# Differential attention, last pair of heads: scores, norms and products in another order among the output projection's units

## The reference, cut

```python
def one(qs):
    a, c = qs
    s1 = jnp.einsum('bhqd,bhkd->bhqk', a, k1).astype(jnp.float32) * scale
    s2 = jnp.einsum('bhqd,bhkd->bhqk', c, k2).astype(jnp.float32) * scale
    p = jax.nn.softmax(s1, axis=-1) - lam * jax.nn.softmax(s2, axis=-1)
    return jnp.einsum('bhqk,bhkv->bhqv', p.astype(v.dtype), v)
...
def post(o):
    return merge_heads(rms_norm(o, subln_g) * (1.0 - lam_init)) @ w_out

yx = post(diff_attend(q1x, q2x, k1a, k2a, va, lam))
...
h_x = h_x + gm * rms_norm(yx, norm_g[l, 1])
fx = conv_ffn(modulate(rms_norm(h_x, norm_g[l, 2]), shf, scf), ...)
```

## Time and profile before

| | us |
|---|---|
| median of 3 runs | 1880.49 (1878.75 to 1881.62) |
| profiled execution | 1877.86 |
| its span, first to last instruction | 1876.1 |
| TensorE busy | 1797.3 |
| VectorE busy | 1142.5 |
| ScalarE busy | 836.0 |
| mean granted clock of TensorE | 0.986 |

### The profile page before, as it was taken

One profiled execution on the slowest core, in us unless ns is written; L12 is line 12 of the kernel. 1 busy time (PEld: TensorE's weight loads), 2 busy tenths in 40 slices (PEclk: granted clock), 3 DMA queues, 4 the chain that ended last, 5 costly groups with the idle time before them and its releaser, 6 DMA issues. The chain is left out here.

```text
span 1876.1 us, 26231 instructions
## 1 busy us (share of the span) xinstructions
PE 1797.3 (96%) x9865; PEld 1501.4 (80%) x9865; DVE 1142.5 (61%) x1523; ACT 836.0 (45%) x1206; POOL 87.0 (5%) x164
## 2 busy tenths in 40 slices
PE   5999999999999999999989999799989999989997
PEld 2877767777678888888878887699879987879985
DVE  2766757667367688644346565566665695755554
ACT  3423233332456432334245555556554546544453
POOL 2000001000000010000000000000001000000000
PEclk8999999999999999999999999899999999999999
DMA  8654545545355476432323223355545554546662
GB/s 290 196 154 143 161 144 151 154 143 159 97 207 186 136 232 184 131 93 97 105 62 107 79 82 99 102 182 185 187 152 183 161 158 146 179 135 186 183 192 100
DMA packets 150910, 282.38 MB, mean 151 GB/s; under 512 B 12652, under 2 KB 78308, under 8 KB 150689
## 3 DMA queue, kind: packets, MB, share of 16 engines
q1 hardware_dynamic: 133344, 220.54, 37.7%
q0 software_dynamic: 17472, 60.57, 10.6%
HBM read 276.83 MB, written 4.23 MB: 150 GB/s over the span
## 5 line engine op out<-in xcount | busy, mean ns | idle before, releaser
L2245 DVE TENSOR_TENSOR wl<-raw,wh 128x1024 fp32r<-128x1024 f32 (+1 forms) x388 | 454.5, 1181 | 379.0 <-ACT wh L1521 376.4
L1521 ACT ACTIVATE wh<-raw 128x1024 fp32r<-128x1024 f32 (+1 forms) x388 | 393.5, 1023 | 614.7 <-PE ps L571 601.5
L569 PE MATMUL ps<-uh,wh 128*128 128x256 f32 (+1 forms) x1216 | 380.7, 313 | 7.3 <-DVE spare L2267 7.3
L570 PE MATMUL ps<-ul,wh 128*128 128x256 f32 (+1 forms) x1216 | 378.9, 312 | 0.0
L571 PE MATMUL ps<-uh,wl 128*128 128x256 f32 (+1 forms) x1216 | 378.8, 311 | 0.0
L569 PE MATMUL ps<-wh,uh 128*128 128x512 f32 (+2 forms) x960 | 368.2, 383 | 9.7 <-issue 6.2
L570 PE MATMUL ps<-wl,uh 128*128 128x512 f32 (+2 forms) x960 | 354.6, 369 | 0.0
L571 PE MATMUL ps<-wh,ul 128*128 128x512 f32 (+2 forms) x960 | 354.3, 369 | 0.0
L569 PEld LDWEIGHTS ps<-uh,wh 128*128 128x128 f32 x1216 | 231.9, 191 | 22.4 <-issue 7.0
L571 PEld LDWEIGHTS ps<-uh,wl 128*128 128x128 f32 x1216 | 231.9, 191 | 12.7
L570 PEld LDWEIGHTS ps<-ul,wh 128*128 128x128 f32 x1216 | 231.9, 191 | 12.3
(11 more groups left out here) (302 smaller groups left out, 1486.9 us busy)
## 6 DMA issues: line engine op xcount, KB each, us to landing
raw<-in_ffn_w_up SPq DMA_DIRECT2D x176, 256.0 KB
arena<-in_ada_w POOLq DMA_DIRECT2D x80, 512.0 KB, 4.2
raw<-in_w_in SPq DMA_DIRECT2D x60, 512.0 KB
raw<-in_ret_w_in SPq DMA_DIRECT2D x48, 512.0 KB
raw<-in_ffn_w_down SPq DMA_DIRECT2D x40, 512.0 KB
raw<-in_ret_w_out SPq DMA_DIRECT2D x32, 512.0 KB
raw<-in_w_up SPq DMA_DIRECT2D x32, 512.0 KB
raw<-in_w_down SPq DMA_DIRECT2D x32, 512.0 KB
```

The source lines that it names most:

```text
L569: pe.matmul(o, lh, rh, start=first, stop=False)
L570: pe.matmul(o, lh, rl, start=False, stop=False)
L1521: T.mark(act.activation(wh[:, j, 0:size], raw[:, j, 0:size], ACT.Copy), hi_done)
L2245: T.mark(vec.tensor_tensor(wl[:, j, 0:size], raw[:, j, 0:size], wh[:, j, 0:size], ALU.subtract), lo_done)
```

## The change

For the last pair (LAST = 3), scores (0, 0) and (0, 1) go ahead of output unit 0, around `values(2)`; `turn_dy(2)` and both scores of head 1 go behind unit 1, with score (1, 0) now in bank 2 and (1, 1) in bank 0 (`score_bank`). The probabilities are turned behind units 2 and 3. The products are taken per head, head 0 behind unit 3 and head 1 behind unit 4, into banks 2 and 3, with a root, a scaling, a transposition (banks 0 and 1) and a pair of high and low parts for each. On ScalarE a function without a reader is called at some places: a root (`roots_next`) ahead of three row norms and behind the last exponents, and an exponential (`exponents_next`) behind the root of pair 2. The reciprocal row sums of the last pair lie in columns of their own (`shares`). On VectorE the helpers `scale_values` and `take_dy` get the heads as a parameter in the same way as on the other engines. Leading blanks are cut, and so are hunks that only pass on the new helpers.

```diff
@@ -343,6 +343,25 @@
 def normed_block(nt, half, b, c):
     x = parts_of(uh, nt, half)[1]
     return x[:, b, c * 256:(c + 1) * 256] if nt == 4 else x[:, 2 * b + c, :]
+def score_bank(i, h, t):
+    return 0 if (h, t) == ((1, 1) if i == LAST else (1, 0)) else 2
+LAST = DH // 2 - 1
+def turned_bank(i, h):
+    return h if i == LAST else 0
+def shares(i, o, n=1):
+    c = (72 if i == LAST else 56) + o
+    return st[:, c:c + n]
+def value_bank(i, h):
+    return 2 + h if i == LAST else h
 def tiles_of(nt, part):
@@ -1097,11 +1116,12 @@
         if (h, t) == (0, 0):
             pe.wait_ge(dqkt_ready, i + 1)
             pe.wait_ge(emptied, values_group[0])
-        elif (h, t) != (1, 0):
-            pe.wait_ge(dexp_done, 4 * i + h + t)
-        elif i:
-            pe.wait_ge(dyt_lo, i)
-        b = heads_v if (h, t) == (1, 0) else heads_v + 2
+        elif score_bank(i, h, t) == 0:
+            if i:
+                pe.wait_ge(dyt_lo, i)
+        else:
+            pe.wait_ge(dexp_done, 4 * i + (2 if (h, t) == (1, 0) else h + t))
+        b = heads_v + score_bank(i, h, t)
         for c in range(2):
             r = slice(64 * c, 64 * c + 64)
             mm = pe.matmul(ps[:, b + c, :], dqt[r, h, t * P:(t + 1) * P], dkt[r, h, :], start=True, stop=True)
@@ -1110,29 +1130,31 @@
     def turn_dprob(i, h, b):
         pe.wait_ge(dprob_ready, 4 * i + 2 * h + 2)
+        if i == LAST:
+            pe.wait_ge(dexp_done, 4 * i + 3 + h)
         for k in range(4):
             for t in range(2):
                 c = (k % 2) * SEQ + t * P
                 mm = pe.transpose(ps[:, b + k // 2, c:c + P], dpr[:, h, t, k * P:(k + 1) * P], ident[:, :])
         mm.then_inc(dprob_turned, 1)
-    def values(i):
-        pe.wait_ge(dpt_ready, 2 * i + 2)
+    def values(i, heads=range(2)):
+        pe.wait_ge(dpt_ready, 2 * i + heads[-1] + 1)
         pe.wait_ge(emptied, values_group[0])
-        for h in range(2):
+        for h in heads:
             for t in range(2):
                 for k in range(4):
-                    mm = pe.matmul(ps[:, heads_v + h, t * P:(t + 1) * P], dpt[:, h, k, t * P:(t + 1) * P],
+                    mm = pe.matmul(ps[:, heads_v + value_bank(i, h), t * P:(t + 1) * P], dpt[:, h, k, t * P:(t + 1) * P],
                                    dvs[i % 2][:, k, h * P:(h + 1) * P], start=k == 0, stop=k == 3)
             mm.then_inc(dvalued, 1)
-    def turn_dy(i):
-        pe.wait_ge(dy_ready, 2 * i + 2)
-        for h in range(2):
+    def turn_dy(i, heads=range(2)):
+        pe.wait_ge(dy_ready, 2 * i + heads[-1] + 1)
+        for h in heads:
             for t in range(2):
-                mm = pe.transpose(ps[:, heads_v, h * SEQ + t * P:h * SEQ + (t + 1) * P], dy[:, h, t, :], ident[:, :])
+                mm = pe.transpose(ps[:, heads_v + turned_bank(i, h), h * SEQ + t * P:h * SEQ + (t + 1) * P], dy[:, h, t, :], ident[:, :])
         mm.then_inc(dy_turned, 1)
     values_group = [0]
@@ -1210,13 +1232,11 @@
             base = S.next() * SLOTS
             for half in (range(0, 2), range(2, 4)):
                 apart = s == 1 and half[0] == 2
-                if apart:
-                    turn_dy(DH // 2 - 1)
                 for z in ((0,), (1,)) if apart else ((0, 1),):
                     for j in half:
                         pe.wait_ge(lo_done, base + j + 1)
                         k = 4 * s + j
-                        pe.wait_ge(dyt_lo, k // 2 + 1)
+                        pe.wait_ge(dyt_lo, LAST + 1 + k % 2 if apart else k // 2 + 1)
                         for t in z:
                             for c in range(2):
                                 mm = three(ps[:, heads_q + 2 * t + c, :], ah8[:, k, t * P:(t + 1) * P], al8[:, k, t * P:(t + 1) * P],
@@ -1242,17 +1262,24 @@
                 pe.wait_ge(dqkt_ready, i + 1)
                 for h in range(2):
                     turn_dprob(i - 1, h, heads_q + 2 * h)
-    last = DH // 2 - 1
+    score(LAST, 0, 0)
+    values(LAST - 1)
+    score(LAST, 0, 1)
     for k in project_heads():
-        if k < 4:
-            attend_early(last, k)
+        if k == 1:
+            turn_dy(LAST - 1)
+            score(LAST, 1, 0)
+            score(LAST, 1, 1)
+        elif k == 2:
+            turn_dprob(LAST, 0, heads_v + 2)
+        elif k == 3:
+            turn_dprob(LAST, 1, heads_v)
+            values(LAST, range(0, 1))
         elif k == 4:
-            pe.wait_ge(dexp_done, 4 * last + 3)
-            turn_dprob(last, 0, heads_v)
-        else:
-            pe.wait_ge(dexp_done, 4 * last + 4)
-            turn_dprob(last, 1, heads_v + 2)
-            values(last)
+            values(LAST, range(1, 2))
+            turn_dy(LAST, range(0, 1))
+        elif k == 5:
+            turn_dy(LAST, range(1, 2))
     turn_normed(2)
     with pe.Fori(0, 5) as i:
         S.enter(i, 2)
@@ -1582,6 +1609,11 @@
             o = part * SEQ
             T.mark(act.activation(ah[:, j, o:o + SEQ], yt[:, 4 * s + j, o:o + SEQ], ACT.Copy), ak_hi)
+    def roots_next():
+        T.settle()
+        T.mark(act.activation(st[:, 71:72], epsc[:, 0:1], ACT.Sqrt), act_own)
     def rms(tiles, src, width, cols, waits=None):
         for t in tiles:
@@ -1885,6 +1917,7 @@
     project(lambda k: hid[:, k, :], TOK, par.now())
     shift0[0] = 0
     layer[0] = 1
+    roots_next()
     act.wait_ge(rows_done, 1)
     for t in range(2):
         square_y(t, side)
@@ -1942,22 +1975,38 @@
         act.wait_ge(dprob_turned, 2 * i + h + 1)
         T.mark(act.activation(dpt[:, h, :, :], ps[:, b:b + 2, :].rearrange("p b (k n) -> p (b k) n", k=2), ACT.Copy), dpt_ready)
-    def rms_values(i):
-        for h in range(2):
+    def square_values(i, heads=range(2)):
+        for h in heads:
             act.wait_ge(dvalued, 2 * i + h + 1)
             for t in range(2):
                 o = 2 * h + t
                 T.settle()
-                T.mark(act.activation(junk[:, 0:P], ps[:, heads_v + h, t * P:(t + 1) * P], ACT.Square,
-                                      scale=st[:, 56 + 2 * o:57 + 2 * o], accum_out=st[:, 16 + o:17 + o]), act_own)
+                T.mark(act.activation(junk[:, 0:P], ps[:, heads_v + value_bank(i, h), t * P:(t + 1) * P], ACT.Square,
+                                      scale=shares(i, 2 * o), accum_out=st[:, 16 + o:17 + o]), act_own)
+    def root_values(heads=range(2)):
         T.settle()
-        T.mark(act.activation(st[:, 20:24], st[:, 16:20], ACT.Sqrt, scale=1.0 / P, bias=epsc[:, 0:1]), drms_done)
-    def take_dy(i):
-        act.wait_ge(dy_turned, i + 1)
-        T.mark(act.activation(ah8[:, 2 * i:2 * i + 2, :], ps[:, heads_v, :].rearrange("p (h n) -> p h n", h=2), ACT.Copy,
+        c = slice(2 * heads[0], 2 * heads[-1] + 2)
+        T.mark(act.activation(st[:, 20:24][:, c], st[:, 16:20][:, c], ACT.Sqrt, scale=1.0 / P, bias=epsc[:, 0:1]), drms_done)
+    def exponents_next():
+        T.settle()
+        T.mark(act.activation(st[:, 70:71], epsc[:, 0:1], ACT.Exp), act_own)
+    def rms_values(i):
+        square_values(i)
+        root_values()
+    def take_dy(i, heads=range(2)):
+        act.wait_ge(dy_turned, i + heads[-1] + 1 if i == LAST else i + 1)
+        k, o = 2 * i + heads[0], heads[0] * SEQ
+        n = len(heads)
+        T.mark(act.activation(ah8[:, k:k + n, :], ps[:, heads_v + turned_bank(i, heads[0]), o:o + n * SEQ].rearrange("p (h n) -> p h n", h=n), ACT.Copy,
                               scale=lamt[:, 5:6]), dyt_hi)
     def attend_early(p, size):
@@ -1987,12 +2036,26 @@
                 take_dprob(i - 1, h, heads_q + 2 * h)
         split(units=range(3, 4))
         take_v(i)
-    last = DH // 2 - 1
-    attend_early(last, UNIT)
+    exponents(LAST, 0, 0)
+    square_values(LAST - 1)
+    exponents(LAST, 0, 1)
+    root_values()
+    exponents_next()
+    split(units=range(0, 1))
+    take_dy(LAST - 1)
+    exponents(LAST, 1, 0)
+    exponents(LAST, 1, 1)
+    roots_next()
+    split(units=range(1, 2))
+    take_dprob(LAST, 0, heads_v + 2)
+    split(units=range(2, 3))
+    take_dprob(LAST, 1, heads_v)
+    split(units=range(3, 4))
     for h in range(2):
-        take_dprob(last, h, heads_v + 2 * h)
-    rms_values(last)
-    take_dy(last)
+        square_values(LAST, range(h, h + 1))
+        root_values(range(h, h + 1))
+    for h in range(2):
+        take_dy(LAST, range(h, h + 1))
     S.base += 2
     finish_rows(2)
     shift0[0] = 24
@@ -2878,10 +2947,22 @@
         take_qk()
         split()
         take_v(i)
-    last = DH // 2 - 1
-    attend_early(last, UNIT)
-    scale_values(last)
-    take_dy(last)
+    row_maxima(LAST, 0, 0)
+    combine(LAST, 0, 0)
+    row_maxima(LAST, 0, 1)
+    combine(LAST, 0, 1)
+    scale_values(LAST - 1)
+    split(units=range(0, 1))
+    take_dy(LAST - 1)
+    row_maxima(LAST, 1, 0)
+    row_maxima(LAST, 1, 1)
+    combine(LAST, 1, 0)
+    combine(LAST, 1, 1)
+    split(units=range(1, 4))
+    for h in range(2):
+        scale_values(LAST, range(h, h + 1))
+    for h in range(2):
```

(27 more changed lines are left out.)

## The result

The changed kernel takes 1867.54 us (median of 4 runs, 1865.66 to 1869.95) against 1879.62 before (4 runs): a ratio of 0.9943, 95% interval 0.9931 to 0.9955, so 8.5 to 13.0 us less; the medians differ by 12.1. The forecast was 8.7 less, from a median of 1880.49 to 1871.8, with a range of 1867.6 to 1876.5.

What follows compares the result with a forecast made beforehand. TensorE, busy 96% of the span, was taken as the bound, losing time to waits and half clock. Gains of 6.1 (last pair), 1.3 and 1.3 us made 8.7, from 1880.49 to 1871.8 us; range 1867.6 to 1876.5.

Steps and rivals of the forecast that it cites:

- The work and its order: Last pair: all TensorE instructions remain, only reordered; 34.3 us at full clock without waits.
- First wait: Last pair, ahead of score (0,0): TensorE waits for VectorE's copy of the values, 3.6 us instead of 0.72.
- Second wait: Last pair, ahead of the turn of pair 2's products: TensorE idles 0.5 us until their scaling ends.
- Third wait: Last pair, ahead of score (1,1): TensorE idles 1.6 us until both copies of pair 2's turned products free bank 0.
- No waits at the heads' norms: Last pair, after score (1,1): TensorE never waits for either head's values, norm or turn; margins 0.15 to 0.8 us, also 1.9.
- The clock behind the first wait: Last pair's first scores and values: half clock costs 2.1 us, bounds 1.65 and 3.4.
- Behind the others: Last pair, behind the waits of 0.5 and 1.6 us: half clock costs 0.5 us, between nothing and 1.65.
- rival with two losses: Last pair: half clock costs 3.4 us and then 1.65, gain 6.2 us, time 1874.3 us; chance 0.16.
- The loads at the norms: Unused roots move table loads into ScalarE's idle time: 1.28 us gained at layer 0's end and layer 1's, nothing last.
- The sum: Whole kernel: 6.1 us from the last pair plus 1.3 and 1.3 from the roots elsewhere, 8.7 us less.

Runs made afterwards that it cites:

- e4: Changed kernel with pair 3's value copies ahead of weight unit 3's split on ScalarE and VectorE: 1863.16 us against 1878.10 before the change, ratio 0.9922.
- e5: Changed kernel with e4's early copies and VectorE's split of unit 4 behind pair 2's low part and head 1's maxima: 1864.12 us, ratio 0.9920 to before.
- e7: Changed kernel without the unused exponential and unused root inside the last pair; one profile: last pair's stretch 40.42 us, 0.5 less than the changed kernel.
- e6: Changed kernel with both heads' products of the last pair taken together behind unit 4, under one norm; one profile: stretch 43.24 us, 2.3 more.
- e2: Changed kernel without the three unused roots ahead of row norms: 1868.31 us against 1878.10 before the change, ratio 0.9946.
- e10: Changed kernel profiled once more, nothing altered: last pair's stretch 42.38 us against 40.93 in its first profile.
- e8: Changed kernel with output unit 0 ahead of the last pair's first scores again; one profile: stretch 39.35 us against 40.93 in the changed kernel.
- e9: Kernel of e8 run again, unchanged; one profile: last pair's stretch 39.31 us.
- e3: Changed kernel with 10 unused identity matmuls in TensorE's first wait of the last pair: 1864.55 us against 1878.10 before the change, ratio 0.9931.

## Why the prediction was right, and where its sizes were off

The order of the waits was forecast rightly. That the sum came out near is in part luck: the pair gave 1.9 us more than forecast, and the root at layer 1's end 1.2 us less.

- *The work and its order* (34.3 us at full clock): right. The stretch of e4 without its waits (1.13, 0.35, 1.05) is 34.4; it ends at ScalarE's square, which lies 0.24 behind the end taken in the prediction.
- *First wait, 3.6 us:* 3.46. e4 shows that 2.3 of it are the two splits ahead of the copies, as said.
- *Second wait, 0.5:* 0.37. *Third wait, 1.6:* 1.05. This step was mis-sized by 0.55. Of it, 0.2 are TensorE's own work: from the turn of pair 2 to the end of score (1,0) it takes 1.72 us (1155.07 to 1156.79), not 1.5. The other 0.35 come from adding full durations along ScalarE and VectorE (exponential table, its dummy, split; split, low part). In the profile ScalarE's split (1154.82) and VectorE's low part (1157.04) each start about 0.1 us before the recorded end of the one ahead, the dummy takes 0.20, not 0.30, and TensorE starts 0.05 behind the low part, not 0.15. e5 and e7 show what the wait was made of: each takes off one split's or one load's delay and gives 0.5.
- *No waits at the heads' norms, with margins of 0.15 to 0.8:* right, in every profile of that order. e6 shows the price of the other way, 2.3.
- *The clock behind the first wait, 2.1, bounds 1.65 and 3.4:* 1.6 and 3.1 in two profiles of the changed kernel, 1.5 to 1.6 in e2, e6 and e7 by the time that score and values took. The term was fair, and the lower bound slightly too high. *Behind the others, 0.5:* nothing in any profile; 0.5 us too much. The rival with two losses fell. The Trainium skill's rule on transpositions ("TensorE: Matmul & The Clock Gate", Part 4: PE-mode transpose) would have had the short waits joined into one (1.65 us); no run here shows a fall there.
- *The loads at the norms, 1.28 + 1.28 + 0:* right at the first and the third place, and at the second only as far as TensorE's wait (2.74 to 1.46). The step that failed is that this 1.28 reaches the end. Behind the shorter wait `keep_clock` runs at full clock and takes 3.74 and not 4.76 us; 0.26 of that reach the mixer, as ScalarE's row is then the later. But TensorE now waits 2.57 and not 2.08 us ahead of the mixer, half clock follows, and the mixer takes 1.48 us longer: 0.05 in place of 1.28. The prediction weighed what the clock does in the pair, and left it out here. Whether the longer wait brings the fall, or that the clock had not just fallen under `keep_clock`, was not tried. The Trainium skill's 2.7 us for a switch ("ScalarE: Activation LUTs", What ACT_TABLE_LOAD costs) is not what this trace has: the load takes 1.28, and the root starts 0.02 behind its end (1151.81 to 1153.11).
- *The sum:* 6.1 + 1.3 + 1.3 = 8.7 forecast, 8.0 + 1.28 + 0.05 = 9.3 by the stages. The pair's 1.9 more are 0.8 of the three waits, 0.5 of the clock behind the first in this profile and 0.5 behind the others; the rest is rounding. The medians give 12.1, and their interval holds 9.3 and 8.7; where the further 2.8 come from isn't shown. With e10's clock the pair gave 6.55, near the 6.1 forecast.

What stays open: the half clock behind a wait. In the 13 profiles it followed some of TensorE's waits of 2 to 5 us behind layer 0 as follows.

| wait, us | followed by half clock |
|---|---|
| 2.08, ahead of the mixer | 0 of 2 |
| 2.35, old order of the pair | 2 of 2 |
| 2.45, behind the pair's row norms | 2 of 13 |
| 2.57, ahead of the mixer | 11 of 11 |
| 2.77, ahead of the last net | 13 of 13 |
| 3.02 to 3.05, late in the mixer | 5 of 13 |
| 3.05 and 3.08, e8 and e9 | 0 of 2 |
| 3.46, new order of the pair | 5 of 5 |
| 4.26, old order of the pair | 2 of 2 |

Every wait of 3.46 us or longer was followed by it, but among the shorter ones length alone doesn't order them: 2.57 always, 3.03 sometimes. The work around them differs, and in e10 the same place cost twice as much as in the first profile; what decides was not tried. So a stretch from a single profile can be off by the 1.5 us between these two prices.

## What to carry to other kernels

When a chain that feeds a dense engine is too late, the gap moves with the reordering but the same work can't cover it twice (4.85 and 4.88 us of waits in e8 and in the changed kernel): count the chain's length against the work that can run beside it, and then look at what stands in the queues ahead of the chain's first signal. Here two weight splits ahead of two copies cost half of what the whole reordering gained (4.0 against 8.0 us), and swapping them brought no other wait (e4). A function table can be brought in early by a call without a reader where the engine idles ahead of a wait that ends on the critical path: at layer 0's end that gave 1.28 us. At layer 1's end the wait fell as well, and the clock took the gain back in the next stage. Where the load already lies beside a longer wait, the call only delays the next work (0.5 us in e7).

## What was not expected of the hardware

- Up to the first row norm of layer 0 the executions of identical code differ by up to 6 us (962.7 to 968.7), with the granted clock of the first stage at 0.85 in one and 0.78 in another. That is as much as half of the effect measured here, so stages were compared inside a profile.
- A gain can be taken back a stage later. The root at layer 1's end brought TensorE to the mixer 1.53 us earlier, and half clock behind a wait of 2.57 us took 1.48 of it, in each of 11 profiles. A stage has to be read to behind the next full-clock stretch, and not only to where the next work begins.
- TensorE at half clock is not a fixed price of a wait: 1.6 and 3.1 us behind the same 3.46 us, nothing behind 3.05 and 3.08. Filling 2.4 us of the gap with identity matmuls took it to nothing (e3).
